# Second layer's modulation vectors: from 96 matmuls on TensorE to scaled and added weight rows on GpSimd, with one sum over the partitions per group

## The reference

```python
def modulation(cond, w_mod, b_mod):
    return jnp.split(jax.nn.silu(cond) @ w_mod + b_mod, 6, axis=-1)

for i in range(DEPTH):                       # DEPTH = 2, D = 1024; w_mod[i] is 1024 x 6144
    need_ctx = i < DEPTH - 1
    sh1_l, sc1_l, gt1_l, sh2_l, sc2_l, gt2_l = modulation(c, w_mod[i], b_mod[i])
    sh1_c, sc1_c, gt1_c, sh2_c, sc2_c, gt2_c = modulation(c_ctx, w_mod[i], b_mod[i])
    h_l = xl * (1.0 + sc1_l) + sh1_l
    h_c = xc * (1.0 + sc1_c) + sh1_c
    ...                                      # attention of h_l and h_c; the ffn of both in layer 0
```

## Time and profile before

| | |
|---|---|
| median of three runs | 1642.85 us |
| span of the profiled execution | 1641.9 us |
| TensorE busy | 1581.9 us (96%) |
| VectorE busy | 828.0 us (50%) |
| ScalarE busy | 735.2 us (45%) |
| GpSimd busy | 0.9 us |
| DMA, mean over the span | 175 GB/s |

### The profile page before, as it was taken

How to read it: one execution, slowest core, us unless ns; L and a number is a source line. 1 busy time by engine, 2 the same in 40 slices (tenths; PEclk the granted TensorE clock), 3 DMA queues, 4 the chain that set the end, 5 groups by cost and what they waited for, 6 DMA issues and landing times.

```text
span 1641.9 us, 27059 instructions
## 1 busy us (share of the span) xinstructions
PE 1581.9 (96%) x11296; PEld 1223.5 (75%) x11296; DVE 828.0 (50%) x1461; ACT 735.2 (45%) x1140; POOL 0.9 (0%) x5
## 2 busy tenths in 40 slices
PE   8999989999999999999989999999999999999987
PEld 5646567777787778789858999998988788535443
DVE  2536664644434444543575756665677675212223
ACT  3545552633212332443463744546545542554444
POOL 0000000000000000000000000000000000000000
PEclk9999999999999999999999999999999999999999
DMA  9412632244334442422212446452442237799995
GB/s 390 157 39 82 212 118 103 103 181 178 124 120 154 166 162 96 180 77 103 78 36 94 158 151 218 148 174 107 163 143 99 82 131 314 298 407 420 421 421 205
DMA packets 43133, 287.91 MB, mean 175 GB/s; under 512 B 4848, under 2 KB 6000, under 8 KB 12160
## 3 DMA queue, kind: packets, MB, share of 16 engines
q1 hardware_dynamic: 42832, 285.99, 46.4%
q10 hardware_dynamic: 144, 0.06, 0.0%
q0 software_dynamic: 32, 0.07, 0.0%
HBM read 285.05 MB, written 1.05 MB: 174 GB/s over the span
## 4 chain that ended last, share of the span: by engine, by line
PE 82%; DVE 7%; ACT 5%; DMA 4%; issue 1%; SPq 0%; DVEq 0%; ACTq 0%
PE ps L539 17%; PE ps L541 16%; PE ps L540 16%; PE ps L2966 7%; DMA deep<-wts 4%; PE ps L590 2%; DVE WL L524 2%; PE ps L2826 1%; PE ps L1569 1%; PE ps L1540 1%; PE ps L1471 1%; PE ps L708 1%; PE ps L1648 1%; PE ps L1647 1%; PE ps L1646 1%
## 5 line engine op out<-in xcount | busy, mean ns | idle before, releaser
L539 PE MATMUL ps<-HH,WH 128*128 128x512 f32 (+2 forms) x1424 | 470.9, 331 | 10.1 <-DVE WL L524 5.7
L541 PE MATMUL ps<-HH,WL 128*128 128x512 f32 (+2 forms) x1424 | 459.9, 323 | 0.0
L540 PE MATMUL ps<-HL,WH 128*128 128x512 f32 (+2 forms) x1424 | 459.4, 323 | 0.0
L524 DVE TENSOR_TENSOR WL<-ring,WH 128x2048 fp32r<-128x2048 f32 (+2 forms) x134 | 281.5, 2103 | 143.5 <-ACT WH L514 143.4
L539 PEld LDWEIGHTS ps<-HH,WH 128*128 128x128 f32 x1424 | 270.0, 190 | 54.7 <-issue 22.5
L514 ACT ACTIVATE WH<-ring 128x2048 fp32r<-128x2048 f32 (+2 forms) x134 | 236.0, 1763 | 153.2 <-PE ps L541 76.6
L541 PEld LDWEIGHTS ps<-HH,WL 128*128 128x128 f32 x1424 | 270.0, 190 | 20.4
L540 PEld LDWEIGHTS ps<-HL,WH 128*128 128x128 f32 x1424 | 270.4, 190 | 18.4
L2966 PE MATMUL ps<-deep,arena 128*32 128x512 f32 (+1 forms) x872 | 114.4, 593 | 10.7 <-ACT late_x L2952 5.6
L539 PE MATMUL ps<-parts,WH 128*128 128x512 f32 (+1 forms) x352 | 119.9, 341 | 0.0
L540 PE MATMUL ps<-parts,WH 128*128 128x512 f32 (+1 forms) x352 | 118.4, 336 | 0.0
(11 more groups left out here) (401 smaller groups left out, 2185.3 us busy)
## 6 DMA issues: line engine op xcount, KB each, us to landing
ring<-wts SPq DMA_DIRECT2D x138, 1024.0 KB, 4.9
deep<-wts SPq DMA_DIRECT2D x92, 1024.0 KB, 16.3
ring<-wts SPq DMA_DIRECT2D x32, 704.0 KB, 4.0
arena<-wts SPq DMA_DIRECT2D x8, 1024.0 KB, 15.6
ring<-wts SPq DMA_DIRECT2D x4, 672.0 KB, 13.7
X<-xin SPq DMA_DIRECT2D x4, 512.0 KB, 16.5
ahead<-wts SPq DMA_DIRECT2D x2, 1024.0 KB, 8.5
deep<-wts SPq DMA_DIRECT2D x4, 512.0 KB, 20.5
```

The source lines that it names most:

```text
L524: e.tensor_tensor(lo, raw(i), hi.bitcast(F32), ALU.subtract).then_inc(*up("low", i))
L539: e.matmul(o, w[0][:, cols], x[0], start=k == 0, stop=False)
L540: e.matmul(o, w[0][:, cols], x[1], start=False, stop=False)
L541: return e.matmul(o, w[1][:, cols], x[0], start=False, stop=k == nk - 1)
```

## The change

The 96 matmuls of layer 1's 24 chunks and the turns of its three groups go. A modulation chunk of layer 1 now holds 512 output columns of one of twelve groups g and half of the 1024 rows (i = 0 or 1, four blocks of 128 rows side by side). GpSimd multiplies each 512-column block with the condition's value of its row and adds the blocks. For groups 0 to 3 (the first shift and scale) it does so twice, for the context as well as the latents: `mod_streams` is then two long. TensorE sums each finished group over the partitions with four matmuls against ones, ScalarE copies the sums to `mrow`, and TensorE turns them with two matmuls (g below 4) or one. The ring slot of such a chunk is freed by GpSimd's last addition for it.

```diff
-MODS_FIRST, MODS_LAST = range(3), range(21, 24)
-MOD_AT = {f: f + 1 for f in range(2, 20)}
+MOD_CHUNKS = {("gu", 1): (0, 1, 2), **{("gu", f): (f + 1,) for f in range(2, 11)}, ("down", 1): (12,), ("down", 3): (13,),
+              **{("gu", f): (f + 3,) for f in range(11, 21)}}
+MOD_SUMS_AT = {2: 0, 3: 1, 5: 2, 7: 3, 8: 4, 10: 5, 11: 6, 12: 7, 14: 8, 16: 9, 18: 10, 20: 11}
...
+    if kind == "mod" and key[1]:
+        g, i = divmod(key[2], 2)
+        return pack_k(x["w_mod"][1][512 * i:512 * i + 512, 512 * g:512 * g + 512])
...
+        mod_tmp = cst[:, cat["cos96"][0]:cat["cos96"][0] + 512]
+        def pool_mods(e):
+            e.wait_ge(*at("mrow.cond"))
+            e.wait_ge(*at("variance.mean", "n00"))
+            for c in range(24):
+                g, i = divmod(c, 2)
+                n = index["mod", 1, c]
+                if g >= 2 and i == 0:
+                    e.wait_ge(*at("modT.sums", g - 2))
+                e.wait_ge(*landed(n))
+                w = raw(n).rearrange("p (k f) -> p k f", k=4)
+                if len(mod_streams(g)) > 1:
+                    for k in range(4):
+                        o = mod_part(g, 0) if k + 4 * i == 0 else mod_tmp
+                        if k or i:
+                            e.wait_ge(*at("mod_acc.sum", g, 4 * i + k - 1))
+                        e.tensor_scalar(o, w[:, k, :], mod_by(4 * i + k, 0), None,
+                                        ALU.mult).then_inc(*up("mod_acc.sum" if k + 4 * i == 0 else "mod_acc.scaled", g, 4 * i + k))
+                        if k or i:
+                            e.wait_ge(*at("mod_acc.scaled", g, 4 * i + k))
+                            e.tensor_tensor(mod_part(g, 0), mod_part(g, 0), mod_tmp,
+                                            ALU.add).then_inc(*up("mod_acc.sum", g, 4 * i + k))
+                x = mod_streams(g)[-1]
+                for k in range(4):
+                    t = e.tensor_scalar(w[:, k, :], w[:, k, :], mod_by(4 * i + k, x), None, ALU.mult)
+                t.then_inc(*up("mod_acc.product", c))
+                e.wait_ge(*at("mod_acc.product", c))
+                e.tensor_tensor(w[:, 0:2, :], w[:, 0:2, :], w[:, 2:4, :], ALU.add).then_inc(*up("mod_acc.pairs", c))
+                e.wait_ge(*at("mod_acc.pairs", c))
+                o = mod_part(g, x)
+                if i == 0:
+                    e.tensor_tensor(o, w[:, 0, :], w[:, 1, :], ALU.add).then_inc(*up("mod_acc", c))
+                else:
+                    e.tensor_tensor(w[:, 0, :], w[:, 0, :], w[:, 1, :], ALU.add).then_inc(*up("mod_acc.whole", c))
+                    e.wait_ge(*at("mod_acc.whole", c))
+                    e.tensor_tensor(o, o, w[:, 0, :], ALU.add).then_inc(*up("mod_acc", c))
+
+        def pe_mod_sums(e, g):
+            pe_mod_end(e)
+            b = bank(e, "mod", 1, g)
+            q = mod_width(g)
+            e.wait_ge(*at("mod_acc", 2 * g + 1))
+            for j in range(4):
+                x, a = divmod(q * j, 512)
+                t = e.matmul(ps[32 * j:32 * j + 32, b, 0:q], C("ones", 32), mod_part(g, x)[:, a:a + q], start=True, stop=True)
...
-                    if l == 0 and f in MOD_AT:
-                        pe_mod(e, 1, MOD_AT[f])
+                    if l == 0:
+                        if f in MOD_SUMS_AT:
+                            pe_mod_sums(e, MOD_SUMS_AT[f])
+                        else:
+                            pe_mod_end(e)
...
+            if key[0] == "mod" and key[1]:
+                return at("mod_acc", key[2])
```

More of the change, by code:

```diff
@@ L193, in ffn_plan @@
             p.append((("gu", l, f), 2048))
-            if l == 0 and f == 1:
-                p += [(("mod", 1, c), 2048) for c in MODS_FIRST]
-            if l == 0 and f in MOD_AT:
-                p.append((("mod", 1, MOD_AT[f]), 2048))
-        p += [(("down", l, half, j), HALF * 128) for j in range(8)]
+            if l == 0:
+                p += [(("mod", 1, c), 2048) for c in MOD_CHUNKS.get(("gu", f), ())]
+        for j in range(8):
+            p.append((("down", l, half, j), HALF * 128))
+            if (l, half) == (0, 0):
+                p += [(("mod", 1, c), 2048) for c in MOD_CHUNKS.get(("down", j), ())]
     return p
@@ L516, in dve_low @@
         def dve_low(e, n, ahead=2):
-            short = plan[n][0][0] == "gu" and n + 1 < len(plan) and plan[n + 1][0][0] == "mod"
+            short = plan[n][0][0] in ("gu", "down") and n + 1 < len(plan) and plan[n + 1][0][0] == "mod"
             for i in range(low_at[0], min(n + (3 if short else ahead), len(plan))):
@@ L602, in pe_mod_end @@
                 e.wait_ge(*at("mrow", l, g))
-                for m in range(4):
+                for m in range(mod_width(g) // 128 if l else 4):
                     t = e.matmul(ps[:, b, 8 * m:8 * m + 8], mrow[:, 128 * m:128 * m + 128], cond[:, 16:24], start=True,
@@ new lines, in pe_mod_sums @@
+        def pe_mod_sums(e, g):
[6 more added lines that the diff above has]
+                t = e.matmul(ps[32 * j:32 * j + 32, b, 0:q], C("ones", 32), mod_part(g, x)[:, a:a + q], start=True, stop=True)
+            t.then_inc(*up("modT.sums", g))
+            banks.give(b, "mrow", 1, g)
+            pe_rows.append((1, g))
@@ new lines, in act_mod_sums, with dve_mod_columns @@
+        def act_mod_sums(e, g):
+            q = mod_width(g)
+            e.wait_ge(*at("modT.sums", g))
+            if act_rows[0]:
+                e.wait_ge(*at("modT", *act_rows[0]))
+            e.activation(mrow[:, 0:q], B("mod", 1, g)[:, 0:q], ACT.Copy).then_inc(*up("mrow", 1, g))
+            act_rows[0] = (1, g)
+        def dve_mod_columns(e, g):
+            bm = cond[:, 72 + 4 * g:76 + 4 * g]
+            e.wait_ge(*at("modT", 1, g))
+            if g < 4:
+                o = modv[1][:, 4 * g:4 * g + 4, :].rearrange("p (h m) s -> p h m s", h=2)
+                x = B("modT", 1, g)[:, 0:16].rearrange("p (m s h z) -> p h m s z", m=2, s=2, h=2)[:, :, :, :, 0]
+                bm = bm.rearrange("p (h m) -> p h m", h=2).unsqueeze(3).to_broadcast([128, 2, 2, 2])
+            else:
+                o = modv[1][:, 4 * g:4 * g + 4, 0]
+                x = B("modT", 1, g)[:, 0:8].rearrange("p (t z) -> p t z", z=2)[:, :, 0]
+            if g // 2 in (1, 4):
+                t = e.scalar_tensor_tensor(out=o, in0=x, scalar=1.0, in1=bm, op0=ALU.add, op1=ALU.add)
+            else:
+                t = e.tensor_tensor(o, x, bm, ALU.add)
+            t.then_inc(*up("mod_ready.sum", 1, g))
@@ L640, in modulation @@
         def modulation(l, v):
+            if l:
+                return at("mod_ready.sum", 1, 2 * v + 1)
             return at("mod_ready.one" if v in (1, 4) else "mod_ready.sum", l, v // 2)
@@ L685, in dve_fold @@
             e.wait_ge(*modulation(l, sh // 8))
-            for s in range(2):
+            for s in range(1 if tag == "n10" else 2):
                 e.tensor_tensor(fold[:, s, :], V(f"{gname}{lg}", 0, 8), modv[l][:, sc:sc + 8, s], ALU.mult)
@@ L739, in pe_moments, with pe_norm @@
                 banks.give(b[1], "variance", tag)
-        def pe_norm(e, N, between=(), warm=None):
+        def pe_norm(e, N, warm=None):
             b = bank(e, "mean", N.tag)
@@ L745, in pe_norm @@
             banks.give(b, "scaled.centered", N.tag, 7)
-            for c in between[:1]:
-                pe_mod(e, 1, c)
             b = bank(e, "unit_dev", N.tag)
@@ L754, in pe_norm @@
             banks.give(b, "scaled", N.tag, 7)
-            for c in between[1:]:
-                pe_mod(e, 1, c)
         def act_shift(e, N):
@@ L1000, in act_ffn @@
                         put_off.pop(0)()
-                    if l == 0 and f in MOD_AT:
-                        act_mod(e, 1, MOD_AT[f])
+                    if l == 0 and f in MOD_SUMS_AT:
+                        act_mod_sums(e, MOD_SUMS_AT[f])
                 act_out(e, ("down", l, half), 1, F_.tag if half else None)
@@ L1034, in dve_ffn @@
                         dve_low(e, c, 3)
[L1035 to L1038, removed]
+                    if l == 0:
+                        dve_mod_end(e)
+                        if f in MOD_SUMS_AT:
+                            dve_rows.append((1, MOD_SUMS_AT[f]))
                 if half and fold_next:
@@ L3418, in _ @@
         def _(e):
-            pool_program(e)
+            run("POOL", pool_program, e)
         @block.scalar
```

31 lines of the change are left out of this document (19 added, 12 removed).

## The result

The changed kernel takes 1745.53 us (median of 4 runs, 1743.65 to 1747.14) against 1642.45 us before: ratio 1.062 (95% interval 1.061 to 1.064), 103 us slower. Slower was forecast, at 1672.2 us with 1712 as the upper end; the time lies outside the range. The profiled execution has a span of 1741.7 us, 99.8 us over that of before.

The account below looks back on a forecast made before the run. TensorE, busy 96% of the span, was taken as the bound; 14.3 us would be saved if nothing waits. With GpSimd's chunk at 16.5 us, 8 x 16.5 - 102.6 = +29.4 us, so 1672.2 us, range 1634 to 1712.

Parts of the forecast that it names:

- The mechanism: Feed-forward stage of layer 0: gu 8's load waits for GpSimd's eighth chunk, so block 8 starts no earlier than 297.7 + 8c.
- 8 x 0.69: Eight 512-column scalings in a GpSimd chunk of groups 0 to 3, each at VectorE's pace of 0.69 us.
- c: GpSimd's time for one chunk of groups 0 to 3, two streams; forecast 16.5 us.
- 8c - 102.6: Change of the kernel's time in us for c above 11.0; +29.4 at c = 16.5, turning at 12.8.
- GpSimd's start: GpSimd begins its first chunk when the mean is there, at 288.60 us.
- From the free slot to TensorE: From issue of gu 8's load to end of its split: 4.84 landing, 1.92 high, 2.29 low part; 9.1 us.
- The clock in block 8: No clock is lost on TensorE, as waits for DMA up to 21 us were still granted 1.00.
- Behind block 8: After block 8, 10.2 us are won back; one-stream chunks take 7.7 us, under a block's 11, so GpSimd keeps up.
- The saving itself: TensorE loses 24.9 us of work and gets 10.6 us of sums and turns: 14.3 us if nothing waits.
- slow in all it does: Rival: GpSimd at half VectorE's pace throughout, c = 20.4, ten more blocks late, +80 us, 1723 us; chance 0.08.
- The exclusion: Rival: GpSimd stands still while VectorE runs with two SBUF operands; c = 18.8, +47.8 us, 1690.6 us; chance 0.17.
- My bounds for c: Additions and scalings at VectorE's pace give c = 10.2 us, at half of it 20.4.

Follow-up runs that it names:

- The runs that change GpSimd's work: Changed kernel without the context's share on GpSimd: 1655.66 us, ratio 1.0074; changed kernel with scalings as tensor_tensor products with a stride-0 factor: 1701.63 us, ratio 1.035.
- the run with the later split: Changed kernel with the split of gu 3 on ScalarE and VectorE taken in block 2 instead of ahead of block 1's work: 1742.84 us, ratio 1.0605.
- little work on GpSimd: Changed kernel with every GpSimd scaling and addition cut to 8 columns, loads, waits and TensorE's sums kept: 1633.29 us, ratio 0.9935 to the kernel before.
- load-only run: Kernel before plus 166 GpSimd scalings and additions of the changed kernel's widths that nothing waits for until block 21 is done: 1643.45 us, ratio 0.9997.
- the probes: Kernel before with 27 probe instructions and two memsets on GpSimd on a free area, each waiting for the one ahead: 1646.80 us, a single run.

## Why the prediction was wrong

The mechanism was right: `gu 8` waits for `mod 7`'s slot, and the time goes with 8c. The step that failed is the term "8 x 0.69": I gave GpSimd VectorE's pace for scalings "since they bring one operand", and no row showed GpSimd at such work. A scaling takes 1.56 us, more than the addition, and this is the very opposite of what I argued.

| part of c, us | predicted | measured |
|---|---|---|
| 8 scalings of 512 | 5.5 | 12.5 (8 x 1.56) |
| 5 additions of 512 | 6.9 | 6.4 (5 x 1.27) |
| 1 addition of 1024 | 2.4 | 2.4 |
| gaps between dependent steps | 1.0 | 0.7 |
| blocked by VectorE | 0.7 | 1.6, as the rest |
| c | 16.5 | 23.6 |

With c = 23.6 the formula 8c - 102.6 gives 86 us, where 99.8 were measured. Point by point, against the predicted +29.4:

- c itself: 8 x (23.583 - 16.5) = +56.6 us. The runs that change GpSimd's work show it: c from 23.6 to 12.5 gave 90 us, and to 19.4 gave 44, of which 34 are the eight chunks.
- GpSimd's start: 286.9 instead of 288.6, -1.7 us. It began right behind the copy of the mean, as predicted, but this execution reached the copy at 286.40 where that of before did at 288.31. It is no effect that I can name: the run with the later split, the same up to there, began GpSimd's work at 288.15.
- From the free slot to TensorE: 10.8 instead of 9.1 us, +1.7. L528 took 3.94 us in it instead of 2.29, beginning while L686 ran.
- The clock in block 8: +2.7 us. The prediction put the clock at nothing, for waits for DMA of up to 21 us that had left it at 1.00. The earlier trace rows show no such wait: in their second window TensorE was busy 56.82 of 60 us, and its longest wait for DMA in that whole trace was 8.0 us. So the zero had no ground. Here TensorE stood 10.0 us in front of block 8, and its first matmuls ran at 1.2 GHz.
- Behind block 8: +11.1 us, which is what the others leave of the miss. One-stream chunks take 12.7 us on average, not 7.7, mostly the scaling again (4 x 1.56 = 6.2 where I had 2.8). They are longer than a block, and TensorE stood 5.8 us at four sums. Behind the last of these waits block 21 took 12.4 us instead of 10.8, at the lower clock, and behind the norm after it the clock cost some 1.5 us more. The last 2 us I cannot place.

The line of the waits at the sums, from 487 to 745 us, is the second of these:

```profile
PE ps L543 <- DVE WL L528: 10.0, 1, 10.0
PE ps L703 <- POOL arena L694: 5.8, 4, 2.6
```

The five points sum to 70.4 us, the miss, since the last one was taken as the remainder. The saving itself was close: 14.3 predicted, 11.5 of the span measured with little work on GpSimd. The difference is 1 us for the sums and some 3 us for the clock behind the two norms, less about 1 us that I cannot place.

Of the rivals, "slow in all it does" came nearest, with c = 20.4 and 1723 us at a chance of 0.08. It was still 22 us short: it had the scaling at 1.38 us instead of 1.56, and 20 us of late blocks where TensorE's waits at the sums were 5.8. The exclusion exists. The Trainium skill, "SBUF — State Buffer", "Who interferes with whom", says that two such instructions do not share the port pair: the one issued first has it to its end, and the other stands. The traces agree on both sides: L528 began at 482.34 during L686 (which ended at 484.12) and took 3.94 us, and the addition behind it began during L528 and took 3.21 where 1.27 is usual.

```profile
481.78 2.34 POOL L686 TENSOR_TENSOR ring<-ring 128x1024 f32<-128x1024 f32 x1
484.21 3.21 POOL L690 TENSOR_TENSOR arena<-ring 128x512 f32<-128x512 f32 x1
```

But in the load-only run, where nothing waits for GpSimd, it cost nothing. My bounds for c, 10.2 to 20.4, came from VectorE's rows and did not hold 23.6: a factor of two over another engine was not an upper bound.

## What to carry to other kernels

Ask of work that is moved to an idle engine how long it holds what others need, not how long that engine is idle: 300 us beside TensorE cost nothing when they held nothing, and 189 us that held ring slots cost nearly all that went beyond TensorE's pace. In such a place compare the time per chunk of the new consumer with the time per block of the engine it feeds; one that is slower by a little in every block costs that little each time. And where the trace has no row for an operation on an engine, probe it or take the forecast's upper end well past twice the neighbour. Last, ask what stood where the work is taken away: here matmuls that only filled a wait kept TensorE's clock at full speed for the blocks behind it.

## What the runs showed of the hardware

- GpSimd's `tensor_scalar` takes 1.56 us for 512 columns, with a constant factor about the same; the probes had 0.93, 1.57 and 2.85 us for 256, 512 and 1024. Its `tensor_tensor` addition takes 1.27 us for 512 and 2.34 for 1024; a `tensor_tensor` product with a stride-0 factor 1.04 us for 512 and 3.60 for 2048. The Trainium skill, GPSIMD Engine Reference, "Engine selection", calls one-input work "roughly line-rate" there; the scalings measured here are slower than two-input additions, and the measurement decides.
- Of 8 columns a scaling took 0.31 us and an addition 0.20 where nothing held them up; the means, some blocking in them, were 386 and 323 ns.
- TensorE's matmuls were 0.43 us apart instead of 0.227 behind waits of 34.0 and of 10.0 us in the changed kernel. They were so also behind the waits of 2.7 us at the end of the norms in the run with little work, with a granted clock of 0.64 and 0.62, where the kernel before, with 0.87 us of wait left, had 1.00.
